# Latent attention: rotary queries of two heads projected together, the maximum taken negative, the large keys' columns scaled first, and separate orders for even and odd heads

## What is computed

```python
q = (_rmsnorm(q_lat, q_lat_w) @ w_uq).reshape(B, L, MLA_HEADS, MLA_NOPE + MLA_ROPE)     # 128 + 64
kv = (_rmsnorm(kv_lat, kv_lat_w) @ w_ukv).reshape(B, L, MLA_HEADS, MLA_NOPE + MLA_V)    # 128 + 128
q_nope, q_pe = _rmsnorm(q[..., :MLA_NOPE], qn_w), _rope(_rmsnorm(q[..., MLA_NOPE:], qpe_w), cos, sin)
s = q_nope . k_nope + q_pe . k_pe            # k_pe: one rotary key for all heads
p = softmax(s * (MLA_NOPE + MLA_ROPE) ** -0.5)
y = (p @ v) * silu(g_mla)
```

## Time and profile before

| | before |
|---|---|
| median of 3 runs | 1414.36 us (1412.99 to 1416.44) |
| profiled execution | 1412.37 us |
| its span | 1410.6 us, 20322 instructions |
| busy TensorE, VectorE, ScalarE, GpSimd | 1335.9, 777.8, 507.1, 606.6 us |
| mean granted TensorE clock | 0.982 |

### The profile page before, as it was taken

One profiled execution on the slowest core, in us unless ns is written; L12 is line 12 of the kernel. 1 busy time (PEld: TensorE's weight loads), 2 busy tenths in 40 slices (PEclk: granted clock), 3 DMA queues, 4 the chain that ended last, 5 costly groups with the idle time before them and its releaser, 6 DMA issues.

```text
span 1410.6 us, 20322 instructions
## 1 busy us (share of the span) xinstructions
PE 1335.9 (95%) x6862; PEld 1076.8 (76%) x6862; DVE 777.8 (55%) x1507; ACT 507.1 (36%) x1066; POOL 606.6 (43%) x367
## 2 busy tenths in 40 slices
PE   7999999998999999999985899999899999999987
PEld 6877777785888888888874677777677888888865
DVE  4237775645556565511142677777425776666761
ACT  3233334213333333200023566666103444444420
POOL 5423332353444444555530444443265555544411
PEclk9999999999999999999997999999899999999999
DMA  6422222232333333333230111111043322222112
GB/s 177 107 66 76 70 65 75 75 90 61 103 89 99 94 89 101 96 102 95 85 105 16 45 46 31 45 30 45 15 130 89 83 68 64 71 71 70 48 33 69
DMA packets 196560, 105.38 MB, mean 75 GB/s; under 512 B 18982, under 2 KB 194444, under 8 KB 196508
## 3 DMA queue, kind: packets, MB, share of 16 engines
q1 hardware_dynamic: 196060, 104.00, 25.8%
q0 software_dynamic: 432, 0.69, 0.3%
q10 hardware_dynamic: 16, 0.00, 0.0%
HBM read 102.57 MB, written 2.10 MB: 74 GB/s over the span
## 4 chain that ended last, share of the span: by engine, by line
PE 81%; DVE 6%; issue 5%; POOL 3%; ACT 3%; DMA 1%; SPq 0%; DVEq 0%; POOLq 0%; ACTq 0%
PE ps L352 19%; PE ps L353 19%; PE ps L354 18%; PE ps L374 9%; PE ps L1237 2%; PE ps L1248 1%; POOL w_low L339 1%; PE ps L1265 1%; PE ps L1267 1%; PE ps L1266 1%; POOL y_low L660 1%; PE ps L898 1%; POOL sq L641 1%; PE ps L920 1%; PE ps L1291 1%
## 5 line engine op out<-in xcount | busy, mean ns | idle before, releaser
L339 POOL TENSOR_TENSOR w_low<-w_raw,w_high 128x1024 fp32r<-128x1024 f32 x183 | 447.8, 2448 | 547.3 <-DVE w_high L334 547.2
L352 PE MATMUL ps<-h_high,w_high 128*128 128x512 f32 x864 | 352.9, 408 | 11.4 <-DVE h_low L475 8.4
L353 PE MATMUL ps<-h_low,w_high 128*128 128x512 f32 x864 | 343.5, 398 | 0.0
L354 PE MATMUL ps<-h_high,w_low 128*128 128x512 f32 x864 | 341.9, 396 | 0.0
L334 DVE CAST w_high<-w_raw 128x1024 fp32r<-128x1024 f32 x183 | 136.9, 749 | 138.0 <-PE ps L354 74.0
L352 PEld LDWEIGHTS ps<-h_high,w_high 128*128 128x128 f32 x864 | 163.3, 189 | 61.6 <-issue 20.5
L354 PEld LDWEIGHTS ps<-h_high,w_low 128*128 128x128 f32 x864 | 163.7, 189 | 37.6
L353 PEld LDWEIGHTS ps<-h_low,w_high 128*128 128x128 f32 x864 | 163.5, 189 | 35.0 <-issue 1.7
L2054 DVE SCALAR_TENSOR_TENSOR z<-ps,cv,z 128x511 f32<-128x511 f32 x44 | 33.0, 750 | 97.8 <-ACT z L1518 97.8
L1518 ACT ACTIVATE z<-ps,cv 128x512 f32<-128x512 f32 x44 | 34.3, 779 | 121.9 <-PE ps L354 121.7
L354 PE MATMUL ps<-m_high,w_low 128*128 128x512 f32 x176 | 69.4, 395 | 0.0
(11 more groups left out here) (338 smaller groups left out, 2508.7 us busy)
## 6 DMA issues: line engine op xcount, KB each, us to landing
w_raw<-in_w_in_dram SPq DMA_DIRECT2D x150, 256.0 KB, 3.2
w_raw<-in_w_up_dram SPq DMA_DIRECT2D x88, 256.0 KB, 3.2
w_raw<-in_w_out_dram SPq DMA_DIRECT2D x44, 256.0 KB, 3.0
w_raw<-in_w_down_dram SPq DMA_DIRECT2D x32, 256.0 KB, 3.0
w_raw<-in_w_down_dram SPq DMA_DIRECT2D x16, 192.0 KB, 2.6
rel<-in_rel_bias_dram SPq DMA_DIRECT2D x8, 384.0 KB, 3.2
x_tok<-in_x_dram SPq DMA_DIRECT2D x4, 512.0 KB, 5.7
w_raw<-in_w_ob_dram SPq DMA_DIRECT2D x8, 256.0 KB, 2.9
```

Source lines behind the costliest of these rows:

```text
L339: pool.tensor_tensor(w_low[:, n % RING, :], w_raw[:, n % RAW, :], w_high[:, n % RING, :].bitcast(F32), ALU.subtract).then_inc(low_made, 1)
L352: pe.matmul(acc, wh, mh, start=first and k == 0, stop=False)
L353: pe.matmul(acc, wh, ml, start=False, stop=False)
L354: done = pe.matmul(acc, wl, mh, start=False, stop=last and k == tiles - 1)
```

## The change

- The strip of an even head holds, in place of the second copy of its own 64 rotary query columns, those of the next, odd head. `m_project` 0, the squares, `m_sums` 0, `m_root` 0, `m_normed` 0, `m_rotate` and `m_rope` run for even heads alone and prepare both heads in a tile of its own, `q_pe`. Each head then rounds its half (`m_high_of` 1) and VectorE, in place of GpSimd, writes the low part into the other half (`m_pe_low`, semaphore `xp_low`).
- The scale of the softmax goes into the gains of `q_pe` and `q_nope` (`mq_gain`, two instructions in the setup). The maximum is taken with a negative sign, and the ScalarE instruction that negated it is gone.
- `m_scale` scales the 512 large keys' columns first; `m_turn` waits for them, and only its last transpose waits for the 80 meta columns.
- The gate has two buffers `mg`, the gated output its own `gy`. `q_pe` and `gy` lie over slot 7 of `y_high` and `y_low`.
- The calls are ordered anew, in one order for a head followed by an even one and one for a head followed by an odd one. The gate's product is cut 3, 1, 4 for even and 3, 1, 3, 1 for odd heads. `strip_used` is raised after the values' product.

```diff
+                a.enter_context(nc.sbuf_tensor("y_high_", [P, 7, S], F32))
+                q_pe = sb("q_pe", [P, S], F32, a)[:]
+                a.enter_context(nc.sbuf_tensor("y_low_", [P, 7, S], F32))
+                gy = sb("gy", [P, S], F32, a)[:]
...
-                gm = sb("gm", [P, S], F32, a)
+                mg = sb("mg", [P, 2, S], F32, a)
...
-                m_sig = sb("m_sig", [P, S], F32, a)
...
-                        ("twice", 704, 64, q[:, :, bass.ds(i * 96 + g * 192 + 128, 64)])]
+                        ("twice", 704, 64, q[:, :, bass.ds(i * 96 + g * 192 + (320 if g % 2 == 0 else 128), 64)])]
...
-                for item in range(2):
...
+                for item in range(c % 2, 2):
...
-                if item == 0:
-                    dst, src, hi = kn_low[:, c % 2, :], kn_f, kn_high[:, c % 2, :]
-                elif item == 1:
-                    pool.wait_ge(s["x_low"], i * 6 + (3 * c + 1))
-                    dst = qpe_parts[64:P, c % 2, :]
-                    src, hi = q_f[64:P, :], dst
-                else:
-                    dst, src, hi = qn_low[:], q_f[:], qn_high[:]
+                dst, src, hi = ((kn_low[:, c % 2, :], kn_f, kn_high[:, c % 2, :]), None,
+                                (qn_low[:], q_f[:], qn_high[:]))[item]
                 pool.tensor_tensor(dst, src, hi.bitcast(F32), ALU.subtract).then_inc(s["x_low"], 1)
...
                 m_low(i, c + 1, 0)
-                m_low(i, c + 1, 1)
-                pool.wait_ge(s["x_low"], i * 6 + (3 * c + 5))
                 make_low(pool, ahead + 1, i * 4)
...
-            GATE_PART = ((0, 2), (2, 3), (3, 7), (7, 8))
+            GATE_PART = (((0, 3), (3, 4), (4, 8)), ((0, 3), (3, 4), (4, 7), (7, 8)))
...
+                    pe.wait_ge(s["xp_low"], i * 2 + (c + 1))
...
+                pe.wait_ge(s["s_probs"], i * 16 + (8 * c + 2 * t + 2))
                 pe.transpose(ps[0:80, 1, 3 * P:4 * P], me_meta[:, t % 2, :], ident[:])\
...
                 if what == 0:
-                    pe.wait_ge(low_made, i * 4 + (n + 1))
+                    if c % 2:
+                        return
                     if c:
-                        pe.wait_ge(s["p_root"], i * 12 + (6 * c - 1))
+                        pe.wait_ge(s["p_root"], i * 10 + (heads(c, 6, 4) - 1))
                     mm = product(pe, ps[:, 7, :], n, 512 + P, 256, 2, ql)
                 elif what == 3:
-                    pe.wait_ge(s["qr_part"], i * 6 + (3 * c + 1))
+                    if c % 2:
+                        pe.wait_ge(s["p_root"], i * 10 + (heads(c, 6, 4) - 1))
+                    else:
+                        pe.wait_ge(s["qr_part"], i * 3 + (3 * (c // 2) + 1))
                     mm = product(pe, ps[:, 7, :], n, 512, 256, 2, ql)
...
-                mm.then_inc(strip_used if what == 3 else s["p_made"], 1)
+                mm.then_inc(strip_used if what == 2 else s["p_made"], 1)
...
             def m_sums(i, c, item):
...
+                if item < c % 2:
+                    return
...
             def m_rotate(i, c):
-                pe.wait_ge(s["p_normed"], i * 6 + (3 * c + 1))
-                pe.matmul(ps[:, 7, :], rot[:], q_f[:], start=True, stop=True).then_inc(s["qr_turned"], 1)
+                if c % 2:
+                    return
+                pe.wait_ge(s["p_normed"], i * 5 + (heads(c, 3, 2) + 1))
+                pe.matmul(ps[:, 7, :], rot[:], q_pe, start=True, stop=True).then_inc(s["qr_turned"], 1)
...
+            def head_then_even(i, c):
+                m_weigh(i, c - 1, 1)
                 m_project(i, c + 1, 0)
+                m_turn(i, c, 0)
                 m_project(i, c + 1, 1)
-                m_turn(i, c, 0)
+                m_scores(i, c, 1)
                 m_sums(i, c + 1, 0)
-                m_scores(i, c, 1)
+                m_gate(i, c + 1, 0)
+                m_turn(i, c, 1)
                 m_sums(i, c + 1, 1)
-                m_gate(i, c + 1, 0)
                 m_rotate(i, c + 1)
-                m_turn(i, c, 1)
-                m_project(i, c + 1, 2)
                 m_scores(i, c, 2)
                 m_weigh(i, c, 0)
                 m_project(i, c + 1, 3)
                 m_gate(i, c + 1, 1)
                 m_turn(i, c, 2)
+                m_project(i, c + 1, 2)
                 m_sums(i, c + 1, 2)
                 m_scores(i, c, 3)
+                m_gate(i, c + 1, 2)
                 m_turn_v(i, c + 1)
+                m_turn(i, c, 3)
+                m_scores(i, c + 1, 0)
+            def head_then_odd(i, c):
+                if c:
+                    m_weigh(i, c - 1, 1)
+                m_project(i, c + 1, 1)
+                m_turn(i, c, 0)
+                m_project(i, c + 1, 3)
+                m_scores(i, c, 1)
+                m_sums(i, c + 1, 1)
+                m_gate(i, c + 1, 0)
+                m_turn(i, c, 1)
+                m_gate(i, c + 1, 1)
+                m_scores(i, c, 2)
+                m_weigh(i, c, 0)
+                m_project(i, c + 1, 2)
+                m_turn(i, c, 2)
+                m_sums(i, c + 1, 2)
+                m_scores(i, c, 3)
                 m_gate(i, c + 1, 2)
+                m_turn_v(i, c + 1)
                 m_turn(i, c, 3)
...
             def m_expo(i, c, t):
                 act.wait_ge(s["s_top"], i * 8 + (4 * c + t + 1))
-                act.activation(mm_[:, t % 2, 1:2], mm_[:, t % 2, 0:1], ACT.Copy, scale=-MLA_SCALE)\
-                    .then_inc(s["s_neg"], 1)
-                act.wait_ge(s["s_neg"], i * 8 + (4 * c + t + 1))
-                act.activation(halves(me[:, t % 2, :]), wide(0), ACT.Exp, scale=MLA_SCALE,
-                               bias=mm_[:, t % 2, 1:2], accum_out=mm_[:, t % 2, 2:3]).then_inc(s["s_exp"], 1)
+                act.activation(halves(me[:, t % 2, :]), wide(0), ACT.Exp, bias=mm_[:, t % 2, 1:2],
+                               accum_out=mm_[:, t % 2, 2:3]).then_inc(s["s_exp"], 1)
...
             def m_high_of(i, c, item):
...
-                dst, src = ((kn_high[:, c % 2, :], kn_f), (qpe_parts[:, c % 2, :], q_f[:]), (qn_high[:], q_f[:]))[item]
...
+                own = slice(c % 2 * 64, c % 2 * 64 + 64)
+                dst, src = ((kn_high[:, c % 2, :], kn_f), (qpe_parts[own, c % 2, :], q_pe[own, :]),
+                            (qn_high[:], q_f[:]))[item]
                 act.activation(dst, src, ACT.Copy).then_inc(s["x_high"], 1)
...
+            def head_then_even(i, c):
+                m_expo(i, c, 0)
+                y_rounded(i, c - 1)
+                m_keep(i, c + 1, 0)
+                m_copy(i, c, 0)
+                m_keep(i, c + 1, 1)
+                m_expo(i, c, 1)
+                m_root(i, c + 1, 0)
+                m_copy(i, c, 1)
+                m_root(i, c + 1, 1)
+                m_expo(i, c, 2)
+                m_square(i, c + 1)
+                m_copy(i, c, 2)
+                m_high_of(i, c + 1, 0)
+                m_high_of(i, c + 1, 1)
+                m_keep_v(i, c + 1)
+                m_root(i, c + 1, 2)
+                m_expo(i, c, 3)
+                m_high_of(i, c + 1, 2)
+                m_place_v(i, c + 1)
+                m_copy(i, c, 3)
+                m_sigmoid(i, c + 1)
...
+            for k, v in enumerate((V_QPE, V_QN)):
+                dve.tensor_scalar(mq_gain[:, k:k + 1], col(v), MLA_SCALE, None, ALU.mult).then_inc(s["gain_ready"], 1)
...
-                dve.tensor_reduce(mm_[:, t % 2, 0:1], wide(0), AX.XY, ALU.max).then_inc(s["s_top"], 1)
+                dve.tensor_reduce(mm_[:, t % 2, 1:2], wide(0), AX.XY, ALU.max, negate=True).then_inc(s["s_top"], 1)
...
                 dve.wait_ge(s["s_inv"], i * 8 + (4 * c + t + 1))
+                dve.tensor_scalar(me[:, t % 2, 0:4 * P], me[:, t % 2, 0:4 * P], mm_[:, t % 2, 3:4], None, ALU.mult)\
+                    .then_inc(s["s_probs"], 1)
                 dve.tensor_scalar(me_meta[:, t % 2, :].rearrange("p (r m) -> p r m", m=META),
-                                  five(me[:, t % 2:t % 2 + 1, 4 * P:L]), mm_[:, t % 2, 3:4], None, ALU.mult)
-                dve.tensor_scalar(me[:, t % 2, 0:4 * P], me[:, t % 2, 0:4 * P], mm_[:, t % 2, 3:4], None, ALU.mult)\
+                                  five(me[:, t % 2:t % 2 + 1, 4 * P:L]), mm_[:, t % 2, 3:4], None, ALU.mult)\
                     .then_inc(s["s_probs"], 1)
...
-                                (q_f[:], col(V_QN), root[:, 0, 0:S]))[item]
+                if item < c % 2:
+                    return
+                dve.wait_ge(s["p_root"], i * 10 + (heads(c, 6, 4) + 2 * nth(c, item) + 2))
+                dst, gain, r = ((q_pe, mq_gain[:, 0:1], root[:, 0, 0:S]), (kn_f, col(V_KN), root[:, 1, :]),
+                                (q_f[:], mq_gain[:, 1:2], root[:, 0, 0:S]))[item]
                 dve.scalar_tensor_tensor(dst, dst, gain, r, ALU.mult, ALU.mult).then_inc(s["p_normed"], 1)
...
+            def m_pe_low(i, c):
+                dve.wait_ge(s["x_high"], i * 6 + (3 * c + 2))
+                own, other = (slice(h * 64, h * 64 + 64) for h in (c % 2, 1 - c % 2))
```

(70 more changed lines are left out.)

182 lines of the change are left out of this document (84 added, 98 removed).

## The result

The changed kernel takes **1429.7 us** (median of 4 runs, 1429.2 to 1431.4) against 1413.7 for the kernel before, timed beside it: a ratio of 1.0117, 95% interval 1.0105 to 1.0129. The prediction, 1406.8, has the wrong sign, and the time lies outside its range. The profiled execution has a span of 1427.6 us, 17.0 more than before.

A forecast was written before the change was run, and what follows sets the result against it. TensorE, busy 95% of the span, was taken as the bound. 12.6 + 2.7 + 0.45 - 2.1 - 2.6 - 1.2 - 1.05 - 0.75 - 0.5 = 7.6 us gained, 1414.36 to 1406.8; 8-in-10 range 1397 to 1417.

The forecast's parts named there:

- The collisions: Latent stage: VectorE instructions meeting running GpSimd ones end late; four places, costing 2.6, 1.2, 1.05 and 0.75 us.
- What goes from TensorE: Odd heads skip six rotary products, block sum and rotation: 3.16 us a head, 12.6 gained for four.
- What goes with it: TensorE's holes before gate product and rotation (0.32 + 0.36) go in odd heads: 2.7 us gained for four.
- The shorter chain: Query tile's probabilities ready 0.45 us earlier; pays fully only at the last head's fourth transposes, 0.45 gained.
- Even heads lose a filler: Before even heads' scores a gate step is gone; TensorE stands 0.70 us longer in three heads, 2.1 lost.
- Odd heads' second tile: Scaling held behind GpSimd's `w_low`, 1.3 us a head; half taken, 2.6 lost in all.
- `m_pe_low`: Odd heads: subtraction in `w_low`'s shadow before the fourth maximum, 0.6 us a head; half taken, 1.2 lost.
- Even heads, rotation: Norming meets the end of a later `w_low`, rotation stands 0.7 us longer; half, times three, 1.05 lost.
- Even heads, ScalarE: `m_high_of(1)` ahead of other ScalarE work delays the fourth exponential, transposes 0.5 us late; half, times three, 0.75 lost.
- Prologue: Before head 0: more gate products first and `q_pe` low part on VectorE behind a likely `w_low`; 0.5 us lost.
- VectorE is held at `m_pe_low`: Rival: the subtraction waits out a whole GpSimd instruction in every head, giving 1419.7 us; chance 0.13.
- whole gain: Rival: no collision decides and the removed work comes out whole, 13.7 us gained, 1400.7; chance 0.20.

The follow-up runs named there:

- experiment 5: experiment 4 with the prologue's third-strip rounding ahead of the first head's scaled queries, and GpSimd's low part of it ahead of its squares: 1398.8 us.
- experiment 3: Kernel before with only the softmax edits (negative maximum, gain folded into the queries, large scaling ahead of the small one): 1413.1 us.
- experiment 4: Changed kernel with second scaling ahead of the strip's rounding, `m_pe_low` behind the fourth maximum, even heads' fourth strip at the end, GpSimd reordered in odd heads: 1406.1 us.
- experiment 7: Changed kernel with `m_pe_low` and the fourth strip moved as in experiment 4, GpSimd's order too, but the second scaling left behind `w_high`: 1416.0 us.
- experiment 2: Kernel before with `w_high` of the strip ahead moved to just ahead of the second tile's scaling, nothing else: 1431.2 us.

## Why the prediction was wrong

The step that failed is **"The collisions"**, and in it the price of a scaling held behind `w_low` at the second tile: 2.6 us in the sum, for odd heads alone and at half price, against 11.8 us that TensorE waited there (4.88 in four odd heads, 6.96 in three even ones, which the list did not have). Beside it the sum put **TensorE's clock at nothing, without a reason**; it cost about 8.8. The forecast and the measurement lie 23.6 us apart (7.6 gained, 16.0 lost), and five misses make up about that: even heads' second tile 7.0, clock 8.8, the subtraction in even heads 3.2, the prologue 2.8 and odd heads' second tile 2.3.

For the odd heads the place, the blocking instruction and the full price (1.3 a head) were named, and then half was taken because the rows could not say which instruction comes first. They could have said more: `w_low` waits for nothing but `w_high`, which stood ahead of the scaling, and by the prediction's own sum GpSimd was due at 1.3 us and the scaling at 1.76. GpSimd was first in seven heads of seven. The rule of the Trainium skill (SBUF — State Buffer, Who interferes with whom) that the later one "fully blocks" would have taken 2.6 us more from the gain, and the trace agrees with the blocking: 2.28 to 2.60 instead of 0.49.

Point by point:
- **What goes from TensorE (12.6): right.** Putting the six products back cost 1.24 to 1.38 a head against the 1.37 that was read. Without collisions the two periods are 24.7 and 27.9, 52.6 for the pair instead of 55.2.
- **What goes with it (2.7): in part.** The pair gained 2.6 in experiment 5, against 3.16 + 0.68 - 0.70 = 3.14 forecast without collisions; other small waits took the place of the holes (0.64 to 0.66 for `q_f` in an even-preparing head).
- **The shorter chain (0.45): right.** The last head's fourth transposes wait 0.95 instead of 1.41, in experiment 3 as in the changed kernel; in a time it is too small to be told.
- **Even heads lose a filler (0.70 a head): right.** TensorE waits 0.79 for `mp_meta` there in experiments 4 and 5; in the changed kernel 1.84, with the subtraction on top.
- **Odd heads' second tile (1.3 a head, half taken): full in every odd-preparing head**, 1.16 to 1.24.
- **Even heads' second tile: missing from the list.** The order maximum, `w_high`, scaling was written into these heads as well, and `y_low` in front made it dearer, 2.3 a head. I had looked there only at the rotation.
- **`m_pe_low`: all eight held**, 1.72 to 1.75 and once 2.87. In odd-preparing heads the fourth transposes wait 0.61 to 0.62 with it in that place and 0.33 without (experiment 4), about the 0.3 that was taken, which was half of an uncertain 0.6 and so partly luck. In even-preparing heads it added some 1.05 to the wait for the scores (1.84 against 0.79), which the sum did not have and the slower rival had at 1.3.
- **Even heads, rotation (0.35 a head taken): did not come**, since the scaling had taken the block; it came, at 1.03, as soon as the scaling escaped (experiment 7).
- **Even heads, ScalarE (0.25 a head taken): did not come.** The fourth transposes wait 0.41 to 0.44 there in the changed kernel, but not at all in experiment 4, which leaves ScalarE's order as it is.
- **Prologue (-0.5, bound -2): -3.3.** The same collision once more (subtraction 2.87), the copy `q_f` behind it (TensorE waits 3.6), and 6.8 us at half clock from 786.4 on. With the collision out, experiment 5 has its first scores 1.5 us earlier than the kernel before.
- **TensorE's clock: absent from the sum.** 17.6 us more at half clock in the stage are about 8.8 us. That it fell behind the long waits is shown by where the stretches stand and by their going with the waits; why behind some and not behind others stays open.

The stage's length can be checked against experiment 5, whose stage is 26.1 us shorter than the changed kernel's: transposes for probabilities 17.0 - 4.0 = 13.0, scores for `mp_meta` 6.4 - 3.2 = 3.2, half clock 19.5 / 2 = 9.8; together 26.0.

The rival that went to the right side, "VectorE is held at `m_pe_low`" (1419.7), had the queueing right but the wrong chief place: it put 6.4 us more on the subtraction in odd heads, where 0.3 a head is all that it cost. Adding the even heads' second tile (3 x 2.3 = 6.9) gives 1426.6 before any loss of clock. The rival "whole gain" (1400.7) comes near what the change is worth with its collisions moved out of the way, 1398.8, but 1.5 us of that is the prologue, which it had at nothing.

## What to carry to other kernels

When a change puts an instruction that releases GpSimd ahead of a VectorE instruction on the critical chain, price the collision in full wherever GpSimd waits for that release alone. Here it was first in seven heads of seven, and lost only where `y_low` was still running when `w_high` ended (the even heads of experiment 7). List every head or branch into which an order is written, not only the one in which it was noticed, and move the release behind the critical instruction. Two fixes of one chain need not add (17.3 and 13.7 gave 23.6), since each can bring back the same clock, so a fix is judged by what TensorE then waits for next, and a wait of about 2 us that recurs in a stage where TensorE ran at full clock is to be priced above its length: in these runs up to 1.8 us more each.

## What the runs showed of the hardware

- A lead of 0.02 us was enough: `w_low` started at 891.49, the scaling at 891.51, and the scaling lasted until `w_low` was over. Another pair shows both orders: with `y_low` 0.06 us ahead of `w_high` (changed kernel) `w_high` took 1.78, and with `w_high` 0.10 us ahead (experiment 7) it took 0.69 and GpSimd's `y_low` 1.75 instead of 1.29.
- The order of these meetings was the same in every head of the changed kernel: seven of seven scalings held, and eight of eight subtractions. In experiment 7 it was the same in every head of a kind: the scalings held in four odd-preparing heads of four, and behind `w_low` in none of three even-preparing ones.
- A TensorE wait of 1.8 to 2.4 us was followed, five times of six in the changed kernel, by 3.4 us at half clock. In experiment 2 a wait of 2.0 us came once in each of six heads, but only the last four were followed by such a stretch. With no wait over 1.34 us (experiment 7) there was none between the prologue and the last head. A stretch of 3.4 us cost 1.5 us (30.76 against 29.26, experiment 2) to 1.8 (33.46 against 31.67). What decides whether one comes was not settled.
